# Dilated attention with moving values and a ones column, its sums swapped through DRAM, and half-split down weights in the experts

## Chip, cores and metric

The kernel runs on one core of a Trainium2 chip. The metric is the device time of one execution in microseconds, the median of several runs. Every time below is one of the kernel before the change.

## What is computed

One inference layer for 1024 prompt tokens and 8 single-token samples, all in fp32. Two parts of it matter here.

Dilated attention: 12 heads in three groups of 4, with windows (128, 512, 2048) and dilations (1, 4, 16); the three groups' results are joined by their log sums, which is the same as one softmax over the keys of all three.

```python
o = jnp.einsum('bnrhij,bnjrhd->bnirhd', p.astype(v.dtype), vv)     # per group
l = jnp.stack([r[1] for r in outs], axis=0)
w = jax.nn.softmax(l, axis=0)
return jnp.sum(w[..., None].astype(o.dtype) * o, axis=0)           # over the groups
```

Experts: every token goes to 2 of 32 experts, and the sorted tokens are worked off in blocks of 128 rows with one expert each.

```python
return (jax.nn.silu(xi @ w_gate[ei]) * (xi @ w_up[ei])) @ w_down[ei]   # xi: 128 x 1024
```

## The kernel before

The program is a row of stages, each with a barrier behind it: norm and projection, stick-breaking attention with the gates, dilated attention (`dilated`), the samples' attention, merge and residual, routing, experts (`experts`), and a last stage. Each engine has its own program in a stage, and the engines wait for each other by semaphores.

**`dilated`** works on two pairs of heads (a pair has one head in each half of the 128 partitions, `b` = 0 and 1). A pair has 16 units of 128 queries: units 0 to 7 are eight consecutive blocks of the undilated group with one or two key tiles, units 8 to 15 are the classes modulo 4 of each half of the sequence, for the two dilated groups together, with 2 or 4 key tiles. The order is written out by steps `s`: a unit's scores stand at step `score_step(a)`, its exponential 18 steps later (`EXP_LAG`), its transposes at 19 (`TURN_LAG`), its values at 20 and its eviction at 21; pair 1 starts 4 steps after pair 0's last scores. So pair 0's values run beside pair 1's scores.

Scores (L830) go to PSUM banks `S`; VectorE adds the bias, writes `row` and takes each query's maximum (L952). A query is in a different partition in the blocks and in the classes, so the maxima `mst` are exchanged through DRAM (`maxes`, L795 to L804, on SP's queue): the blocks' maxima out and in again by class, then the classes' out and in again by block. Four bytes or four times four at a time are moved. VectorE joins both (L927, L929), ScalarE takes the exponential with the joint maximum (L900). TensorE turns each 128 x 128 tile of `row` into `tp[b]` (L843), VectorE copies head 0's and ScalarE head 1's to `pT` (L935, L893), and TensorE multiplies, with the values as weights (64 columns) and `pT` moving, and once more with 64 columns of ones for the sums (L867). The result is `[64 dims | sums] x queries` in two banks `O`; ScalarE copies the blocks' to `acc` (L886), VectorE adds the classes' (L960). At a pair's end VectorE takes the reciprocal of all sums and multiplies (L964, L966).

All loads are issued by SP ahead of the swaps: 11 for each pair, of which 5 for the values (L779, L783), whose pieces are 512 bytes.

**`experts`** loops over 32 blocks in this run, with a lag of one block between each pair of steps. In a step TensorE does gate(n-1), turns the hidden tile of n-2, up(n-1), turns x of n, and down(n-2). Gate and up are three fp32r matmuls for each product, of operands split into a high part (rounded by ScalarE, L1930) and a low part (the rest, VectorE, L1973):

```python
def products(pe, out, w_high, w_low, m_high, m_low, first, last):
    pe.matmul(out, w_low, m_high, start=first, stop=False)
    pe.matmul(out, w_high, m_low, start=False, stop=False)
    return pe.matmul(out, w_high, m_high, start=False, stop=last)
```

Down is plain fp32 on `hT` and `wd` (L1891): 4 tiles of the hidden width by 2 banks of 512. The gate and up weights have one buffer each in two halves, reloaded as soon as VectorE has made the low part; `wd` has two. SP issues all of these loads, ScalarE issues the results.

Of the kernel before, what the change touches and what calls it, by code (L numbers as in the profile page):

```python
# [671 lines left out]
def dilated(nc, g):  # L672
# [6 lines left out]
    with ctx:  # L679
# [12 lines left out]
        EXP_LAG, TURN_LAG, VALUE_LAG, EVICT_LAG = 18, 19, 20, 21  # L692
# [24 lines left out]
        def keys(u, x, m):  # L717
# [9 lines left out]
        LAST = max(at_evict) + 1  # L727
# [3 lines left out]
        v = sb("v", [P, PAIRS, N_DIL, QT, P])  # L731
# [3 lines left out]
        acc = sb("acc", [P, PAIRS, 2, SEQ])  # L735
        ones = sb("ones", [P, HD])
        mst = sb("mst", [P, PAIRS, 2, UNITS])
        oth = sb("oth", [P, PAIRS, 2, UNITS])
        nm = sb("nm", [P, PAIRS, 2, UNITS])
        dist = row[:, 0, 0:BAND].bitcast(I32)  # L740
# [7 lines left out]
        s_full, row_full, joint_step, nm_full, p_full, tp_full, o_full, oa_read, ob_read, fin = map(sem, (  # L748
            "s_full", "row_full", "joint_step", "nm_full", "p_full", "tp_full", "o_full", "oa_read",
            "ob_read", "fin"))  # L750
        pT_full = [sem(f"pT_full{b}") for b in range(2)]
# [3 lines left out]
        m_in = [sem(f"m_in{p_}") for p_ in range(PAIRS)]  # L755
        ident, zT, ztok, oaT = g["ident"], g["zT"], g["ztok"], g["oaT"]
# [10 lines left out]

        @block.sync
        def _(sp):
            def load_qk(p_, x):  # L770
                c = x * PAIRS + p_
                sp.dma_start(q[:, p_, x, :], zT[c, :, 0:SEQ]).then_inc(qk_in[p_][x], 16)
                sp.dma_start(k[:, p_, x, :], zT[CA + c, :, 0:SEQ]).then_inc(qk_in[p_][x], 16)

            def load_v(p_):
                for x in range(N_DIL):
                    c = 2 * A_W + (x * PAIRS + p_) * P
                    if x == 0:
                        sp.dma_start(v[:, p_, x, :, :], ztok[0:SEQ, c:c + P].rearrange("(t p) n -> p t n", p=P))\  # L779
                            .then_inc(v_in[p_], 16)  # L780
                    else:
                        for h in range(2):
                            sp.dma_start(v[:, p_, x, h * STRIDE:(h + 1) * STRIDE, :],  # L783
                                         ztok[h * HALF:(h + 1) * HALF, c:c + P]
                                         .rearrange("(n r) c -> n r c", r=STRIDE)).then_inc(v_in[p_], 16)

            for p_ in range(PAIRS):
                for x in range(N_DIL):
                    load_qk(p_, x)
                load_v(p_)  # L790
            with nc.allow_non_contiguous_dma(reason="2048 maxima in another order"):
                for p_ in range(PAIRS):
                    sp.wait_ge(row_full, 2 * (p_ * UNITS + QT))
                    for b in range(2):
                        sp.dma_start(nat(p_, 0)[:, b, :], mst[:, p_, b, 0:QT]).then_inc(m_out[p_][0], 16)  # L795
                    sp.wait_ge(m_out[p_][0], 32)
                    for b in range(2):
                        sp.dma_start(by_class(oth, p_)[:, b, :, :], classes(p_, 0)[:, b, :, :]).then_inc(m_in[p_], 16)
                    sp.wait_ge(row_full, 2 * (p_ + 1) * UNITS)
                    for b in range(2):  # L800
                        sp.dma_start(classes(p_, 1)[:, b, :, :], by_class(mst, p_)[:, b, :, :]).then_inc(m_out[p_][1], 16)
                    sp.wait_ge(m_out[p_][1], 32)
                    for b in range(2):
                        sp.dma_start(oth[:, p_, b, 0:QT], nat(p_, 1)[:, b, :]).then_inc(m_in[p_], 16)  # L804

        @block.gpsimd
        def _(pool):
            pool.iota(dist[:, :], pattern=[[-1, BAND]], base=P, channel_multiplier=1).then_inc(drawn, 1)
            pool.memset(ones[:, :], 1.0).then_inc(drawn, 1)
# [10 lines left out]
        def _(pe):  # L820
# [15 lines left out]
            def turn(a):  # L836
                p_, u = place(a)
                for b in range(2):
                    pe.wait_ge(p_full, 2 * a + b + 1)
                    need(pe, pT_full[b], a)  # L840
# [3 lines left out]
                    last.then_inc(tp_full, 1)  # L844

            def values(a):
                p_, u = place(a)
                if u == 0:
                    pe.wait_ge(v_in[p_], 16 * 5)
                for b in range(2):  # L850
                    pe.wait_ge(pT_full[b], a + 1)
                if a >= 2:
                    e_, w = place(a - 2)
                    if w < QT:
                        pe.wait_ge(oa_read, e_ * QT + w + 1)
                    else:
                        pe.wait_ge(ob_read, e_ * QT + w - QT + 1)
                tiles = []
                for x, m in parts(u):
                    for t in range(m):  # L860
                        tiles.append((x, u + 1 - m + t if x == 0 else t * STRIDE + (u - QT) % STRIDE))
                for side in range(2):
# [898 lines left out]
def experts(nc, g):  # L1761
# [6 lines left out]
    with ctx:  # L1768
# [150 lines left out]
        def _(act):  # L1919
# [21 lines left out]
            def step(it, j):  # L1941
# [4 lines left out]
                if one:  # L1946
                    sigmoid(one[0])
# [444 lines left out]
```

## Time and profile before

| | |
|---|---|
| median of 3 runs | 2235.88 us (2226.49 to 2236.38) |
| profiled execution | 2228.89 us, of which the span is 2227.3 us |
| TensorE (PE) busy | 1855.4 us, 83% |
| VectorE (DVE) busy | 1057.1 us, 47% |
| ScalarE (ACT) busy | 800.7 us, 36% |
| mean granted TensorE clock | 0.911 of full |
| dilated attention | 787 to 984.6 us of the span |
| experts, first load to last issue | 1402.9 to 2041 us |

The profile is of one execution. A busy share is an average over all stages; which engine bounds is read stage by stage. PE rows are matmuls, PEld rows the weight loads, SPq, ACTq and POOLq the rows of queues. An fp32 matmul that isn't a transpose shows as two rows.

### The profile page before, as it was taken

The numbers are of one execution on the slowest core, as the hardware profiler recorded it, in microseconds if no ns is written. First come the engines' busy times: TensorE is split into PE (matmuls) and PEld (weight loads), VectorE is DVE, ScalarE is ACT, GpSimd is POOL, SyncE is SP. The second block draws the span as 40 slices with busy tenths as digits, with TensorE's granted clock in tenths as the row PEclk, the third lists the DMA queues.
The fourth block names the chain that finished last, engine by engine and source line by source line (L and its number), as shares of the span: only waits on it lengthen the run. The fifth ranks groups of instructions, "written<-read, shape, count | busy, mean of one in ns | idle before, by whom it ended". The sixth has DMA issues, their size and how long they took to land. (4 is left out here: it accounts for less than half of the span.)

```text
span 2227.3 us, 26881 instructions
## 1 busy us (share of the span) xinstructions
PE 1855.4 (83%) x9852; PEld 1443.3 (65%) x9852; DVE 1057.1 (47%) x1415; ACT 800.7 (36%) x1096; POOL 128.4 (6%) x181
## 2 busy tenths in 40 slices
PE   5999999789999947632498992599999999996698
PEld 4999999777777835431295541466666677773585
DVE  5211211158888733335151224466666666662674
ACT  4111111147666503220040000454555555452454
POOL 0111111100000000010031003000000000001110
PEclk7999999989999978675699995699999999998799
DMA  3443444245221160025354213899999999994620
GB/s 114 116 121 114 131 126 122 92 140 172 67 86 39 39 180 1 1 55 152 99 167 145 76 39 137 354 390 379 381 384 385 382 385 382 382 378 164 224 75 39
DMA packets 165325, 401.73 MB, mean 180 GB/s; under 512 B 25659, under 2 KB 102955, under 8 KB 144772
## 3 DMA queue, kind: packets, MB, share of 16 engines
q1 hardware_dynamic: 146004, 334.32, 41.8%
q0 software_dynamic: 10320, 33.82, 5.3%
q10 hardware_dynamic: 8928, 32.63, 3.6%
q8 instruction: 45, 0.74, 0.1%
q14 instruction: 28, 0.23, 0.0%
HBM read 325.80 MB, written 82.61 MB: 183 GB/s over the span
## 5 line engine op out<-in xcount | busy, mean ns | idle before, releaser
L87 PE MATMUL p_acc<-uh,p_wl 128*128 128x344 f32 x720 | 234.9, 326 | 13.0 <-DVE ul L293 9.0
L89 PE MATMUL p_acc<-uh,p_wh 128*128 128x344 f32 x720 | 230.6, 320 | 0.0
L88 PE MATMUL p_acc<-ul,p_wh 128*128 128x344 f32 x720 | 230.5, 320 | 0.0
L1891 PE MATMUL x_Y<-x_wd,x_hT 128*128 128x512 f32 x512 | 225.1, 593 | 0.8 <-DVE x_hT L1989 0.8
L305 DVE COPY p_zk<-p_tp 128x512 f32<-128x512 f32 (+1 forms) x90 | 44.2, 547 | 304.4 <-PE p_tp L226 304.4
L1973 DVE TENSOR_TENSOR x_wgl<-x_wg,x_wgh 128x2048 fp32r<-128x2048 f32 x64 | 143.9, 2290 | 49.8 <-ACT x_wgh L1930 49.8
L1891 PEld LDWEIGHTS x_Y<-x_wd,x_hT 128*128 128x128 f32 x512 | 95.0, 190 | 108.2 <-issue 107.1
L269 ACT ACTIVATE p_zc<-p_acc 128x344 f32<-128x344 f32 x90 | 41.2, 458 | 321.6 <-PE p_acc L89 321.6
L1973 DVE TENSOR_TENSOR x_wul<-x_wu,x_wuh 128x2048 fp32r<-128x2048 f32 x64 | 143.8, 2289 | 17.8 <-ACT x_wuh L1930 17.8
L87 PEld LDWEIGHTS p_acc<-uh,p_wl 128*128 128x128 f32 x720 | 135.8, 189 | 18.0 <-issue 14.9
L545 PE MATMUL g_acc<-uh,g_wl 128*128 128x344 f32 x384 | 129.1, 336 | 9.3 <-ACT u L576 7.1
L89 PEld LDWEIGHTS p_acc<-uh,p_wh 128*128 128x128 f32 x720 | 136.0, 189 | 0.0
L88 PEld LDWEIGHTS p_acc<-ul,p_wh 128*128 128x128 f32 x720 | 135.8, 189 | 0.0
L1930 ACT ACTIVATE x_wgh<-x_wg 128x2048 fp32r<-128x2048 f32 x64 | 118.8, 1905 | 47.2 <-DMA x_wg<-in_w_gate 47.2
L1505 PE MATMUL r_acc<-r_w,mT 128*128 128x512 f32 (+1 forms) x288 | 127.3, 601 | 10.1 <-DMA r_w<-in_w_out 10.1
L545 PE MATMUL g_acc<-ul,g_wh 128*128 128x344 f32 x384 | 127.4, 332 | 0.0
L545 PE MATMUL g_acc<-uh,g_wh 128*128 128x344 f32 x384 | 126.9, 330 | 0.0
L87 PE MATMUL x_G<-x_wgh,x_xl 128*128 128x512 f32 x256 | 114.0, 445 | 11.5 <-DVE x_xl L1967 11.5
L1930 ACT ACTIVATE x_wuh<-x_wu 128x2048 fp32r<-128x2048 f32 x64 | 118.5, 1901 | 0.3 <-DMA x_wu<-in_w_up 0.3
L1978 DVE TENSOR_TENSOR x_gs<-x_sg,x_G 128x512 f32<-128x512 f32 x32 | 22.1, 689 | 178.6 <-ACT x_sg L1923 178.6
L1505 PEld LDWEIGHTS r_acc<-r_w,mT 128*128 128x128 f32 (+1 forms) x288 | 51.6, 182 | 79.6 <-issue 69.2
L87 PE MATMUL x_U<-x_wuh,x_xl 128*128 128x512 f32 x256 | 102.9, 402 | 0.0
(316 smaller groups left out, 3676.8 us busy)
## 6 DMA issues: line engine op xcount, KB each, us to landing
x_wg<-in_w_gate SPq DMA_DIRECT2D x64, 1024.0 KB, 7.7
x_wu<-in_w_up SPq DMA_DIRECT2D x64, 1024.0 KB, 7.4
x_wd<-in_w_down SPq DMA_DIRECT2D x32, 2048.0 KB, 12.5
x_x<-xs SPq DMA_DIRECT2D x32, 512.0 KB, 11.6
ys<-x_y ACTq DMA_DIRECT2D x32, 512.0 KB, 11.8
zT<-p_zc ACTq DMA_DIRECT2D x30, 516.0 KB, 3.4
p_w<-in_w_in SPq DMA_DIRECT2D x30, 512.0 KB, 5.5
ztok<-p_zk POOLq DMA_DIRECT2D x30, 512.0 KB, 4.6
```

The costliest lines, as they stand in the source:

```text
L87: pe.matmul(out, w_low, m_high, start=first, stop=False)
L88: pe.matmul(out, w_high, m_low, start=False, stop=False)
L89: return pe.matmul(out, w_high, m_high, start=False, stop=last)
L269: act.activation(zc[:, b, s * NS:(s + 1) * NS], acc[b * NSPLIT + s][:, 0:NS], ACT.Copy).then_inc(zc_full, 1)
L305: dve.tensor_copy(zk[0:r, b, t0:t0 + m, :], tp[j % 2][0:r, 0:m, :]).then_inc(zk_full, 1)
L545: last = pe.matmul(acc[grp % 2][:, 0:NS], lhs[:, c % 2, kk, :], rhs[:, kk, t], start=(x == 0), stop=(x == M - 1), skip_group_check=True)
L1505: last = pe.matmul(acc[t % 2][0:r, c * 512:(c + 1) * 512], mT[:, k, t * P:t * P + r], w[:, k, c * 512:(c + 1) * 512], start=(k == 0), stop ...
L1891: last = pe.matmul(Y[c][:, :], hT[:, k, :], wd[:, b, k, c * 512:(c + 1) * 512], start=(k == 0), stop=(k == KF - 1))
L1930: act.activation(wh[:, HALVES[half], :], w[:, HALVES[half], :], ACT.Copy).then_inc(full, 1)
L1973: dve.tensor_tensor(wl[:, s, :], w[:, s, :], wh[:, s, :], ALU.subtract).then_inc(full, 1)
L1978: dve.tensor_tensor(gs[:, :], sg[:, :], G[:, :], ALU.mult).then_inc(gs_full, 1)
```

## The change

In `dilated` the operands of the value matmuls change places: the turned scores are now the weights (128 columns), and the values move, 64 dims with a column of ones beside them (`v` is 130 wide, a ones column at each end, so that each head has 65 columns with one of ones). The result is `queries x (sum, dims)` for each unit, all 32 of which ScalarE copies to `o` (L924). Blocks and classes are no longer added in the accumulator: their sums go to `den`, are swapped through DRAM as the maxima are, added, inverted, and `o` is scaled; then TensorE turns 4 units at a time into `tp[0]`, and VectorE copies (blocks) or adds (classes) into the output. VectorE makes both copies of each turned tile. SP loads only the queries and keys of pair 0; ScalarE's queue issues all the rest.

In `experts` the first two of the four hidden tiles of the down projection are computed like gate and up, in three fp32r matmuls, with high and low parts of `wd` and of the hidden tile; the other two stay fp32.

```diff
-        v = sb("v", [P, PAIRS, N_DIL, QT, P])
+        v = sb("v", [P, PAIRS, N_DIL, QT, WIDE])
@@ dilated, SP
+            for x in range(N_DIL):
+                load_qk(sp, 0, x)
+                swap(0, 0, mst, oth, m_out[0], m_in[0], row_full, 2 * QT, 2 * UNITS)
+                swap(1, 0, mst, oth, m_out[1], m_in[1], row_full, 2 * (UNITS + QT), 4 * UNITS)
+                for p_ in range(PAIRS):
+                    swap(p_, 2, den, osum, n_out[p_], n_in[p_], den_full, 2 * p_ + 1, 2 * p_ + 2)
@@ dilated, TensorE
-                if a >= 2:
-                    e_, w = place(a - 2)
-                    if w < QT:
-                        pe.wait_ge(oa_read, e_ * QT + w + 1)
-                    else:
-                        pe.wait_ge(ob_read, e_ * QT + w - QT + 1)
+                need(pe, o_read, a - 1)
                 for b in range(2):
-                    pe.wait_ge(pT_full[b], a + 1)
+                    pe.wait_ge(tp_read[b], turned[a, b][1] + 1)
+                            last = pe.matmul(O[a % 2][:, h], pT[:, a % 2, b, n * P:(n + 1) * P], v[:, p_, x, at_v, h],
+            def out(p_, n):
+                need(pe, tp_read[0], turned["out", (p_, n)][1])
+                pe.wait_ge(scaled, p_ + 1)
+                for t in range(4):
+                    last = pe.transpose(tp[0][:, t * P:(t + 1) * P], o[:, p_, n * 4 + t, 1:P + 1], ident[:, :])
@@ dilated, ScalarE
+            load_v(act, 0)
+            for x in range(N_DIL):
+                load_qk(act, 1, x)
+            load_v(act, 1)
@@ dilated, VectorE
+                    for b in range(2):
+                        dve.wait_ge(tp_full[b], turned[a, b][1] + 1)
+                        dve.tensor_copy(pT[:, a % 2, b, 0:n], tp[b][:, 0:n]).then_inc(tp_read[b], 1)
+                if s in at_scale:
+                    p_ = at_scale[s]
+                    dve.wait_ge(n_in[p_], 64)
+                    dve.wait_ge(den_full, 2 * p_ + 2)
@@ experts, ScalarE
+            def high_down(n, b, it):
+                act.wait_ge(d_in[b], it * 16 + 16)
+                need(act, d_used, n)
+                for k in range(KS):
+                    act.activation(wdh[:, k, :], wd[:, b, k, :], ACT.Copy).then_inc(dh_full, 1)
@@ experts, VectorE
+            def low_down(n, b):
+                for k in range(KS):
+                    dve.wait_ge(dh_full, n * KS + (k + 1))
+                    dve.tensor_tensor(wdl[:, k, :], wd[:, b, k, :], wdh[:, k, :], ALU.subtract).then_inc(dl_full, 1)
```

VectorE at the start of pair 1's values, where the new wait stands. Before, the turned tiles of head 0 follow the joint maximum (L927, L929) and its reciprocal and product (L964, L966); `u` is the memory that holds the output:

```order
L964 RECIPROCAL d_acc<-d_acc 128x1024
L966 TENSOR_TENSOR u<-d_acc 128x1024
L927 TENSOR_TENSOR d_oth<-d_oth,d_mst 128x32
L929 TENSOR_SCALAR d_nm<-d_oth 128x32
L935 COPY d_pT<-d_tp 128x128
L935 COPY d_pT<-d_tp 128x256 x10
```

After the change, at the same place:

```order
L951 TENSOR_TENSOR d_oth<-d_oth,d_mst 128x32
L953 TENSOR_SCALAR d_nm<-d_oth 128x32
L995 COPY d_den<-d_o 128x2x8
L971 COPY d_pT<-d_tp 128x128 x2
L971 COPY d_pT<-d_tp 128x256 x4
L1001 TENSOR_TENSOR d_den<-d_den,d_osum 128x32
L1003 RECIPROCAL d_osum<-d_den 128x32
L1006 TENSOR_TENSOR d_o<-d_o,d_osum 128x16x128
L959 COPY u<-d_tp 128x512
L971 COPY d_pT<-d_tp 128x256 x2
```

The sum of both `den` (L1001), which waits for pair 0's swapped sums, stands behind three units' copies and ahead of all others.

ScalarE at the end of the experts, from the last but one result on. Before, the results (L1935) and their issues (L1939) are all that is left behind the last sigmoid:

```order
L1923 ACTIVATE x_sg<-x_G 128x512
L1935 ACTIVATE x_y<-x_Y 128x512 x2
L1939 DMA ys<-x_y 128x1024
L1935 ACTIVATE x_y<-x_Y 128x512 x2
L1939 DMA ys<-x_y 128x1024
```

After the change:

```order
L1973 ACTIVATE x_sg<-x_G 128x512
L1990 ACTIVATE x_hh<-x_tph 128x256
L1995 ACTIVATE x_y<-x_Y 128x512 x2
L1999 DMA ys<-x_y 128x1024
L1986 ACTIVATE x_wdh<-x_wd 128x1024 x2
L1990 ACTIVATE x_hh<-x_tph 128x256
L1995 ACTIVATE x_y<-x_Y 128x512 x2
L1999 DMA ys<-x_y 128x1024
```

The last block's down weights are rounded (L1986) behind the result of the block before it.

## Rows read from the trace of the kernel before

**Rows 1.** The page's first line.
```profile
span 2227.3 us, 26881 instructions
```
**Rows 2.** Busy time by stretch: PE, PEld, DVE, ACT, POOL, then granted clock, DMA share, GB/s.
```profile
787.00:813.20 26.20, 18.83 (x96) 12.37 (x96) 17.87 (x81) 0.00 (x0) 2.24 (x7) 0.80 1.02 342
813.20:831.50 18.30, 0.00 (x0) 0.00 (x0) 0.05 (x2) 0.00 (x0) 0.00 (x0) 0.53 0.32 29
831.50:912.00 80.50, 61.14 (x486) 45.49 (x486) 24.02 (x89) 23.36 (x56) 0.00 (x0) 0.79 0.02 1
912.00:921.00 9.00, 0.00 (x0) 0.00 (x0) 8.93 (x7) 0.00 (x0) 0.00 (x0) 0.58 0.16 2
921.00:975.90 54.90, 42.16 (x390) 33.28 (x390) 11.64 (x25) 23.35 (x56) 0.00 (x0) 0.73 0.00 1
975.90:984.60 8.70, 0.00 (x0) 0.00 (x0) 8.38 (x3) 0.00 (x0) 0.00 (x0) 0.64 0.00 0
1430.00:1470.00 40.00, 37.58 (x155) 27.64 (x154) 28.37 (x20) 21.09 (x16) 0.00 (x0) 0.96 1.00 407
1441.00:2023.00 582.00, 582.00 (x2310) 407.74 (x2309) 364.26 (x242) 297.94 (x241) 0.00 (x0) 1.00 0.96 376
```
**Rows 3.** Timeline of one block of the experts: start, length, instruction.
```profile
1714.12 0.39 PE L87 MATMUL x_U<-x_wuh,x_xl 128*128 128x512 f32 x1
1714.35 0.39 PE L88 MATMUL x_U<-x_wul,x_xh 128*128 128x512 f32 x1
...
1717.05 7.03 PE L1891 MATMUL x_Y<-x_wd,x_hT 128*128 128x512 f32 x16
...
1730.10 3.71 ACT L1930 ACTIVATE x_wgh<-x_wg 128x2048 fp32r<-128x2048 f32 x2
```
**Rows 4.** Timeline of the tail of dilated attention.
```profile
976.54 6.55 DVE L964 RECIPROCAL d_acc<-d_acc 128x1024 f32<-128x1024 f32 x1
983.13 1.22 DVE L966 TENSOR_TENSOR u<-d_acc 128x1024 f32<-128x1024 f32 x1
```
**Rows 5.** Timeline of the end of the experts.
```profile
2031.66 7.12 PE L1891 MATMUL x_Y<-x_wd,x_hT 128*128 128x512 f32 x16 [0.80 <-DVE x_hT L1989]
2032.31 0.34 ACTq L1939 DMA_DIRECT2D ys<-x_y  x1
```
**Rows 6.** Timeline of pair 0's scores and first swap, VectorE and SP's queue.
```profile
800.40 0.08 DVE L952 DVE_READ_ACCUMULATOR2_ANT d_mst<- 128x1 f32 x1
...
811.51 3.80 SPq L795 DMA_DIRECT2D maxes<-d_mst  x2
824.83 0.87 SPq L798 DMA_DIRECT2D d_oth<-maxes  x2
...
831.46 0.19 DVE L927 TENSOR_TENSOR d_oth<-d_oth,d_mst 128x32 f32<-128x32 f32 x1 [18.25 <-DMA d_oth<-maxes]
```
**Rows 7.** Waits of SP's queue, 787 to 935: total, times, longest.
```profile
SPq L798 <- DMA maxes<-d_mst: 19.5, 2, 10.0
```
**Rows 8.** Timeline of TensorE in a wide unit of pair 1.
```profile
963.72 1.09 PE L843 MATMUL d_tp<-ident,d_row 128*128 128x128 f32 x8
965.85 1.09 PE L867 MATMUL d_O<-d_pT,d_v 128*64 128x128 f32 x16 [1.03 <-DVE d_acc L960]
...
967.74 1.09 PE L843 MATMUL d_tp<-ident,d_row 128*128 128x128 f32 x8
```
**Rows 9.** Timeline of the router: a narrow matmul on 128-column weights.
```profile
1323.32 1.87 PE L1522 MATMUL r_lg<-r_wr,r_u2T 128*128 128x36 f32 x16
```
**Rows 10.** The page's groups: weight loads of 128 fp32 columns.
```profile
L1891 PEld LDWEIGHTS x_Y<-x_wd,x_hT 128*128 128x128 f32 x512 | 95.0, 190 | 108.2 <-issue 107.1
```
**Rows 11.** Waits of the dilated stage, 787 to 985.
```profile
PE d_O L867 <- DVE d_acc L960: 17.5, 12, 2.3
```
**Rows 12.** Timeline of TensorE in wide units of pair 0.
```profile
897.01 1.98 PE L867 MATMUL d_O<-d_pT,d_v 128*64 128x128 f32 x16 [2.25 <-DVE d_acc L960]
...
905.72 1.15 PE L867 MATMUL d_O<-d_pT,d_v 128*64 128x128 f32 x16 [2.25 <-DVE d_acc L960]
```

More of the change, by code:

```diff
@@ L755, in dilated @@
         m_in = [sem(f"m_in{p_}") for p_ in range(PAIRS)]
+        n_out = [[sem(f"n_out{p_}{n}") for n in range(2)] for p_ in range(PAIRS)]
+        n_in = [sem(f"n_in{p_}") for p_ in range(PAIRS)]
         ident, zT, ztok, oaT = g["ident"], g["zT"], g["ztok"], g["oaT"]
@@ L787, in _, with swap @@
[L787 to L791, printed above, removed]
-                for p_ in range(PAIRS):
[L793 to L804, printed above, removed]
+            def swap(p_, at, src, dst, out_sems, in_sem, ready, first, second):
+                for b in range(2):
+                    if b == 0:
+                        sp.wait_ge(ready, first)
+                    sp.dma_start(nat(p_, at)[:, b, :], src[:, p_, b, 0:QT]).then_inc(out_sems[0], 16)
+                sp.wait_ge(out_sems[0], 32)
+                for b in range(2):
+                    sp.dma_start(by_class(dst, p_)[:, b, :, :], classes(p_, at)[:, b, :, :]).then_inc(in_sem, 16)
+                sp.wait_ge(ready, second)
+                for b in range(2):
+                    sp.dma_start(classes(p_, at + 1)[:, b, :, :], by_class(src, p_)[:, b, :, :]).then_inc(out_sems[1], 16)
+                sp.wait_ge(out_sems[1], 32)
+                for b in range(2):
+                    sp.dma_start(dst[:, p_, b, 0:QT], nat(p_, at + 1)[:, b, :]).then_inc(in_sem, 16)
@@ L806, in _ @@
+            for x in range(N_DIL):
+                load_qk(sp, 0, x)
+            with nc.allow_non_contiguous_dma(reason="2048 maxima and sums in another order"):
+                swap(0, 0, mst, oth, m_out[0], m_in[0], row_full, 2 * QT, 2 * UNITS)
+                swap(1, 0, mst, oth, m_out[1], m_in[1], row_full, 2 * (UNITS + QT), 4 * UNITS)
+                for p_ in range(PAIRS):
+                    swap(p_, 2, den, osum, n_out[p_], n_in[p_], den_full, 2 * p_ + 1, 2 * p_ + 2)
         @block.gpsimd
@@ L1941, in step @@
             def step(it, j):
-                one, three = lag(it, j, 1), lag(it, j, 3)
+                one, two, three = lag(it, j, 1), lag(it, j, 2), lag(it, j, 3)
                 new = it * 2 + j
@@ L1993, in step @@
                 new = it * 2 + j
+                if two:
+                    low_down(two[0], two[1])
                 if one:
@@ L2007, in end @@
                 last = np_ * 2 - 1
+                low_down(last - 1, 0)
                 gated(last)
@@ L2010, in end @@
                 hidden(last)
+                low_down(last, 1)
                 hidden_T(last)
```

197 lines of the change are left out of this document (120 added, 77 removed).

## The prediction

> **What bounds the kernel now.** I read the page first, then the busy time by stage, then the waits and the timeline of the two stages that the change touches. The span is 2227.3 us [rows 1] and the profiled execution took 2228.9 us, so 1.6 us lie around the span; the sum below is made against 2228.9. The three timed runs lie between 2226.5 and 2236.4, so it stands at their lower side. Less than about 0.5% (11 us) can't be told from no change.
>
> The stages follow one another with a barrier between them, so each is read alone [rows 2]. Dilated attention takes 197.6 us in six pieces: scores of pair 0 while its inputs stream in (26.2), an idle stretch with neither TensorE nor VectorE at work (18.3), pair 0's values beside pair 1's scores (80.5), a turnaround with only VectorE busy (9.0), pair 1's values (54.9), and a tail with only VectorE (8.7). No engine is full in any of them: it is a chain of short hand-overs. The experts stage is the opposite: from 1441 to 2023 TensorE is busy for 582.0 of 582.0 us at full granted clock, with a DMA share of 0.96. TensorE ends each block there, and DMA stands right behind it.
>
> **Experts.** A block has 76 rows of TensorE (48 for gate and up, 12 transposes, 16 for the down projection); 2310 rows in 582 us [rows 2] are 30.4 blocks, so a block takes 19.1 to 19.2 us. The down projection takes 7.03 us for 16 rows: 8 fp32 matmuls of 512 columns, two rows each, 0.44 us a row [rows 3]. The fp32r rows of the same width start 0.23 us apart [rows 3]. The change turns 4 of the 8 fp32 matmuls into 3 fp32r rows each: 4 x (2 x 0.437 - 3 x 0.227) = 0.77 us less per block, and 24.6 us over 32 blocks if TensorE stays the bound.
>
> What is added runs on ScalarE, two copies of 1024 (3.71 us for two of 2048 [rows 3], so 0.95 each) and one of 256 (0.35), and on VectorE, two subtractions of 1024 (a product of 1024 took 1.22 [rows 4], I take 1.2) and one of 256 beside a copy of half size (0.4 more). Per block ScalarE is idle for 9.3 us and VectorE for 7.2 (busy 297.9 and 364.3 of 582 us, over 30.4 blocks) [rows 2]; 2.3 and 2.8 us fit. The down weights' pieces stand at a step's start, where both engines wait for the gate product. The hidden tile's 0.35 us stands ahead of the next gate weights' rounding; the work that hides it is TensorE's up projection and transposes, which never waited. Without that cover it would cost 0.35 x 32 = 11 us, which goes into the range.
>
> At the stage's end the cover is gone. The last block's down weights can be rounded only once the block before has let go of the single buffer, and ScalarE first copies out that block's result and issues it, at 2032.3; before, the last down projection had begun at 2031.7 [rows 5]. Now come, from 2032.6, 0.95 + 0.95 us of copies, 0.35 for the hidden part and two VectorE steps of 0.4 with their hand-overs: 2037.1, so 5.4 us more. TensorE has by then idled over 6 us, and in the dilated stage's idle stretch the granted clock was 0.53 [rows 2], hence the last projection starts at half clock: 7 us of work, some 2.5 us longer. Experts: -24.6 + 5.4 + 2.5 = -17 us.
>
> Can DMA follow? 376 GB/s [rows 2] over 19.2 us are 7.2 MB a block; at 18.43 us that asks for 392 GB/s. The stretch from 1430 to 1470 moved 407 [rows 2], which would allow 17.7 us. So it fits, by 0.7 us.
> The Trainium skill (DMA: Bandwidth & Descriptors, Specifications) gives a core about 358 GB/s of HBM. The trace's 376 over 582 us is already above it. By the page's figure nothing could be won in this stage; by the row all of it.
>
> **Dilated attention, piece by piece.**
> *Loads and the first swap.* SP issued the first half of pair 0's maxima only at 811.5, behind 22 loads, though unit 7 had been reduced at 800.5; it read back at 824.8, and VectorE went on at 831.5, 6.6 us after [rows 6]. With the other loads on ScalarE's queue, SP is free for it at 800.5. The transfer has a latency of its own: SP waited 10.0 us for it once and 9.5 the other time, one of the two with nothing else under way [rows 7]. So it lands at 811 at the earliest and at 824.8, as before, at the latest. From the other side, the scores end at 813.2 and the second half needs 5.7 us: 819. I take 822.5 for VectorE's start, nearer the early end: -9 us (-12 to 0). That the scores begin perhaps 1 us later, since value rows share the DMA engines with the first keys, is in it.
>
> *Matmuls of the values.* Before, a unit of four tiles took 1.9 us at full clock in 32 rows [rows 8]. Now there are half as many matmuls, 65 columns wide, each with its own 128-column fp32 weights. The nearest rows are the router's: 36 columns on 128-column weights, 16 rows in 1.87 us [rows 9]. So 16 rows in 1.9 to 2.2 us: no gain, no loss. The bound above is a load that isn't hidden, 0.19 us a row [rows 10], so 3.0 us.
>
> *Pair 0's loop, 80.5 us.* The gain is a wait. In a wide unit (8.7 us) TensorE stands 2.25 us ahead of the values, because VectorE copies, reduces two score tiles and then adds into the accumulator; this wait came to 17.5 us in 12 places [rows 11, 12]. Now ScalarE empties the bank, and the first head's values begin after VectorE's first copy. For four wide units I count 2.2 us each, for the three ahead of them 1.9, and 0.2 for the others: -16 us (-8 to -20).
> *Turnaround, 9.0 us.* The reciprocal of 1024 (6.55) and the product (1.22) are gone [rows 4]; the swap's second half remains, 6.2: -3.
> *Pair 1's loop, 54.9 us.* A wide unit takes 4.0 us, 2.1 of them from the start of the turns to the values [rows 8]; now 3.6. With the other units that is -5. Against it: SP swaps the sums of pair 0 only after pair 1's maxima are through. The same chain, 10 + 1 + 3 + 3 us, ends some 20 us after the last score reduction. VectorE comes to this wait after the third unit, some 14 us after that reduction; queued behind it are all turned tiles, so TensorE stands 6 to 7 us. Then a sum, a short reciprocal and a product over 2048 (2 x 1.22) take 3 us, and four output tiles add transposes and a copy each, 1.9 us, through the one bank that also turns head 0: +7.6. Of these 17, 2 lie beside values: +15 - 5 = +10 us (+3 to +14; +3 if the transfer of scattered words is quick).
> *Tail, 8.7 us.* The last sums go out and come back, 5.7 us behind an eviction and a copy (0.8), then 3 us of scaling, then four times turn and copy with nothing beside it, 8: 17.5, so +9 us (+6 to +12).
> Dilated: -9 - 16 - 3 + 10 + 9 = -9 us.
>
> **Sum:** -17 - 9 = -26, so 2203 us.
>
> **Rivals.** *DMA is the bound in the experts stage.* For it: a share of 0.96, and only 0.7 us of room above. Against it: 407 GB/s in one stretch, and a TensorE that never waits for weights. The blocks stay at 19.2 us, only the end's 8 us are paid, and with -9 the time is 2228. I give it 0.17. The skill's 358 GB/s would be this case.
> *The weight loads of the values aren't hidden.* At 0.19 us a row against 0.12, 312 rows (156 tiles, two rows each) cost 22 us on TensorE's chain: 2225. At the stage's granted 0.79 [rows 2] it is 0.24 a row, 37 us, 2240: slower. It decides from 0.20 a row on, where the 26 us are eaten. Against it stand the router's rows. 0.08, of which 0.06 slower.
> *The swaps are quick:* the 10 us aren't paid where SP no longer stands behind loads. Then 3 us at the first, 7 at pair 0's sums, and 2 of the tail: 2191. 0.15.
> *The change doesn't do what it says in the dilated stage:* TensorE's wait for the accumulator only moves to the second copy of a turned tile on VectorE, which now makes both. Then the loops give 6 instead of 21 us, and the time is 2218. 0.10.
> My forecast has 0.50.
>
> **How the numbers follow.** The forecast's own terms span about 2192 to 2215. With the 11 us of the hidden part, the DMA case at 2228 and the quick swaps at 2191, 8 in 10 lie between 2182 and 2229. Faster by over 0.5% (under 2218): 0.50 + 0.15 + half of the 0.10, and 0.07 of the DMA case, where the blocks gain a part: 0.77. Slower: 0.06 and a little of the rest, 0.07. Within 0.5%: 0.16.
>
> **What would show it.** Blocks of 18.4 us with TensorE still full; idle time with DMA as releaser would be the first rival. The start and the granted clock of the last down projection. In the dilated stage: VectorE's joint maximum 35 us from the stage's start and not 44; wide units of pair 0 at 6.3 us; a wait of VectorE for the sums' return, 6 us long, after pair 1's third unit; a tail of 17 us; value rows 0.12 us apart at full clock.
> The prediction is wrong if blocks stay at 19.2 us, or if value rows stand 0.19 us apart.

## The result

The changed kernel takes 2243.3 us (median of 11 runs, 2235.0 to 2250.8), the kernel before 2230.8 in the same rounds (2223.7 to 2236.4): ratio 1.0062, 95% interval 1.0045 to 1.008. It is slower by 0.6%, where 2203 was forecast and 0.07 was given to slower.

The page's first line, against [rows 1]:
```profile
span 2239.3 us, 26891 instructions
```
Busy time by stretch of the changed kernel, against [rows 2]: loads and first swap, pair 0's loop, turnaround, pair 1's loop, tail, and most of the experts.
```profile
788.20:832.00 43.80, 19.05 (x96) 12.28 (x96) 18.36 (x82) 0.00 (x0) 2.39 (x10) 0.69 0.88 217
832.00:914.50 82.50, 77.55 (x330) 60.17 (x330) 27.63 (x97) 18.64 (x48) 0.00 (x0) 0.53 0.02 1
914.50:920.70 6.20, 0.00 (x0) 0.00 (x0) 0.51 (x5) 0.00 (x0) 0.00 (x0) 0.63 0.37 4
920.70:993.40 72.70, 54.40 (x250) 46.82 (x250) 20.39 (x42) 18.38 (x48) 0.00 (x0) 0.54 0.05 1
993.40:1010.40 17.00, 4.43 (x16) 2.86 (x16) 5.76 (x8) 0.26 (x1) 0.00 (x0) 0.54 0.08 1
1470.00:2023.00 553.00, 553.00 (x2391) 422.83 (x2390) 433.86 (x328) 364.21 (x328) 0.00 (x0) 1.00 0.98 392
```
The dilated stage grew from 197.6 to 222.2 us. Pair 0's loop is the row to look at: TensorE now works 77.6 of 82.5 us (61.1 of 80.5 before), so the wait for the accumulator is gone, and yet nothing was won, because the granted clock, whose two levels are 0.50 (1.2 GHz) and 1.00 (2.4 GHz), fell from 0.79 to 0.53 over the loop (the experiments below show that this is the cause). It stood at 0.50 up to the loop's last wide unit, for 77 us:
```profile
832.00:909.00 77.00, 73.25 (x306) 57.10 (x306) 24.53 (x89) 18.36 (x47) 0.00 (x0) 0.50 0.02 1
```
In pair 1's loop it fell from 0.73 to 0.54, and TensorE is idle for 18 of 72.7 us.

Timeline of the changed kernel, in the order of time: start, length, instruction, in brackets the idle time ahead and who ended it. These answer to [rows 6], [rows 12], [rows 3] and [rows 5].
```profile
802.80 1.00 SPq L809 DMA_DIRECT2D maxes<-d_mst  x2
825.06 0.88 SPq L812 DMA_DIRECT2D d_oth<-maxes  x2
825.98 0.98 SPq L815 DMA_DIRECT2D maxes<-d_mst  x2
831.80 0.19 DVE L951 TENSOR_TENSOR d_oth<-d_oth,d_mst 128x32 f32<-128x32 f32 x1 [16.43 <-DMA d_oth<-maxes]
...
893.73 3.65 PE L884 MATMUL d_O<-d_v,d_pT 128*128 128x65 f32 x16
...
918.56 1.20 SPq L809 DMA_DIRECT2D maxes<-d_den  x2
929.62 0.88 SPq L812 DMA_DIRECT2D d_osum<-maxes  x2
939.86 1.09 PE L893 MATMUL d_tp<-ident,d_o 128*128 128x128 f32 x4 [10.40 <-DVE d_o L1006]
991.37 1.97 PE L884 MATMUL d_O<-d_v,d_pT 128*128 128x65 f32 x16 [0.51 <-DVE d_pT L971]
...
1718.18 3.59 PE L1941 MATMUL x_Y<-x_wd,x_hT 128*128 128x512 f32 x8
2037.70 2.00 ACT L1986 ACTIVATE x_wdh<-x_wd 128x1024 fp32r<-128x1024 f32 x2 [1.23 <-issue]
2041.87 0.80 PE L87 MATMUL x_Y<-x_wdh,x_hl 128*128 128x512 f32 x1 [6.05 <-DVE x_hl L2059]
2042.46 0.63 PE L88 MATMUL x_Y<-x_wdl,x_hh 128*128 128x512 f32 x1
```
The same 16 value rows take 3.65 us at 893.7 and 1.97 at 991.4: the second stands in the one stretch of that loop where the clock is up. 1.97 lies within the 1.9 to 2.2 forecast from the router's rows [rows 9]. SP issued the first maxima 8.7 us sooner than before, but they were back only at 825.1, against 824.8 [rows 6]. Pair 0's sums go out at 918.6, behind pair 1's maxima, and cost TensorE 10.4 us. The experts did what was forecast: with TensorE full, 2391 rows in 553 us at 80 rows a block (48, 12, 12 and 8) are 18.5 us a block against 19.2, at 392 GB/s. At their end TensorE stands 6.05 us, and the next rows start 0.43 us apart instead of 0.23.

### The profile page after: what moved, and what is told of

Same layout as the page of the kernel before. It is cut to its first block and busy times, and to the rows that moved or that the text cites. A ratio compares the mean times of both kernels' runs of the same rounds, so it can differ in the third digit from the quotient of the medians.

```text
span 2239.3 us, 26891 instructions
## 1 busy us (share of the span) xinstructions
PE 1872.7 (84%) x9700; PEld 1502.3 (67%) x9700; DVE 1135.9 (51%) x1541; ACT 863.7 (39%) x1176; POOL 128.6 (6%) x184
## 5 line engine op out<-in xcount | busy, mean ns | idle before, releaser
L87 PE MATMUL p_acc<-uh,p_wl 128*128 128x344 f32 x720 | 234.8, 326 | 13.5 <-DVE ul L293 9.3
L2041 DVE TENSOR_TENSOR x_wul<-x_wu,x_wuh 128x2048 fp32r<-128x2048 f32 x64 | 143.8, 2289 | 17.8 <-ACT x_wuh L1980 17.8
L1941 PE MATMUL x_Y<-x_wd,x_hT 128*128 128x512 f32 x256 | 115.0, 592 | 0.0
L2064 DVE TENSOR_TENSOR x_wdl<-x_wd,x_wdh 128x1024 fp32r<-128x1024 f32 x64 | 75.5, 1221 | 77.5 <-ACT x_wdh L1986 77.5
L88 PE MATMUL x_G<-x_wgl,x_xh 128*128 128x512 f32 x256 | 101.2, 395 | 0.0
```

The costliest lines, as they stand in the source:

```text
L1941: last = pe.matmul(Y[c][:, :], hT[:, k - KS, :], wd[:, b, k, cols], start=False, stop=(k == KF - 1))
L2041: dve.tensor_tensor(wl[:, s, :], w[:, s, :], wh[:, s, :], ALU.subtract).then_inc(full, 1)
L2064: dve.tensor_tensor(wdl[:, k, :], wd[:, b, k, :], wdh[:, k, :], ALU.subtract).then_inc(dl_full, 1)
```

## The experiments

Sixteen kernels. "Before" was timed beside each; its medians lie between 2229.5 and 2233.3. "Joint" is VectorE's joint maximum, which opens a pair's loop; the loops below run from it to the pair's last value row. "-" and "+" are against the changed kernel where nothing else is said.

### Which part lost the time

**e1_experts_only.** The kernel before with the changed function `experts`.
```diff
-        hT = sb("hT", [P, KF, P])
+        KS = KF // 2
+        wdh, wdl = (sb(n, [P, KS, D], F32R) for n in ("wdh", "wdl"))
```


> The kernel before, with the experts' part of the change alone (gate and up untouched, half of each down projection split into high and low parts). By the two traces the experts' stage is 15.5 us shorter in the changed kernel (618.5 us against 634.0), and all that it loses it loses in dilated attention. If the two parts act apart, this kernel takes about 2231 - 15 = 2216 us, ratio 0.993. Rival: part of those 15.5 us came to the experts from the stages ahead of them (a later start with loads already under way), then it gains less than 10 us, ratio above 0.9955.

Measured: 2216.8 us, ratio 0.9931 (0.9903 to 0.9958), so -15 us against the kernel before. The parts act apart.

**e2_dilated_only.** The changed kernel with the function `experts` of before.
```diff
-        KS = KF // 2
-        wdh, wdl = (sb(n, [P, KS, D], F32R) for n in ("wdh", "wdl"))
+        hT = sb("hT", [P, KF, P])
```


> The kernel before, with the dilated part of the change alone; the experts as before. If the parts act apart, it takes 2243 + 15 = 2258 us, ratio to the kernel before 1.012, and its dilated stage is the 222 us of the changed kernel, with the granted clock at 0.53 in both loops. Rival as for the first kernel: the parts are not independent, and the ratio lies below 1.008.

Measured: 2258.2 us, ratio 1.0129 (1.0099 to 1.0159): the whole loss lies here. The clock of its loops was 0.59, not 0.53, and from the first joint maximum to the last output copy it took 173.5 us in the execution profiled (178.4 in the changed kernel's): with the same instructions the clock rose some 15 us sooner in pair 0's loop here.

### The clock

**e3_columns_130.** Each value matmul moves both heads' columns; the eviction picks.
```diff
-                            last = pe.matmul(O[a % 2][:, h], pT[:, a % 2, b, n * P:(n + 1) * P], v[:, p_, x, at_v, h],
+                            last = pe.matmul(O[a % 2][:, b * WIDE:(b + 1) * WIDE], pT[:, a % 2, b, n * P:(n + 1) * P], v[:, p_, x, at_v, :],
```


> The changed kernel, with each value matmul moving all 130 columns of its value tile (both heads and both ones columns) and not the 65 of its own head; the eviction picks the right 65 out of each half, so the output is the same. Theory: TensorE stays at half clock through both loops because the value matmuls keep it too little at work in the array (65 moved columns behind a weight load, 0.243 us a row). Then the granted clock of the loop over pair 0 rises from 0.53 to 0.7 or more, a value row costs 0.22 to 0.25 us at either width of time, transposes and scores run at double speed for part of the loop, and the kernel takes 2210 to 2235 us, less than the changed kernel in spite of twice the moved columns. Rival: the clock hangs on something else (the stage's rhythm, what went before the loop). Then it stays at 0.53, a value row of 130 columns takes about 0.43 us, 78 rows a pair cost 0.19 us more each, and the kernel takes 2243 + 30 = 2273 us.

Measured: 2212.9 us, ratio 0.9912 (0.9882 to 0.9942). Twice the moved columns, 30 us less. Busy time of e3's two loops, and one narrow unit of its timeline:
```profile
834.50:894.00 59.50, 51.95 (x324) 39.34 (x324) 26.11 (x95) 18.37 (x47) 0.00 (x0) 0.92 0.02 1
903.80:966.20 62.40, 39.84 (x250) 33.99 (x250) 20.23 (x43) 18.37 (x47) 0.00 (x0) 0.77 0.06 1
```
```profile
859.70 0.66 PE L868 MATMUL d_tp<-ident,d_row 128*128 128x128 f32 x4
860.81 1.13 PE L884 MATMUL d_O<-d_v,d_pT 128*128 128x130 f32 x8 [0.46 <-DVE d_pT L972]
```
The clock is back at 0.92 and 0.77, pair 0's loop takes 59.5 us instead of 79.5. Eight rows of 130 columns take 1.13 us at full clock; eight of 65 take 1.08 (next run): the second 65 columns are nearly free there.

**e5_warm_before_loop.** 65 columns; extra matmuls in the first swap's wait.
```diff
+                if at_joint.get(s - 2, -1) in (0,):
+                    warm((18, 2)[0])
+                    pe.wait_ge(m_in[at_joint[s - 2]], 64)
+                    warm((18, 2)[1])
```
Here `warm(n)` is n matmuls of `q[:, 0, 0, 0:512]` by `ident` into `tp[1]`.

> The changed kernel with 65 moved columns, and 20 extra matmuls (fp32, 512 moved columns, result never read) on TensorE while it waits for pair 0's first swap: 18 at once and 2 more when the swap has landed. They bring TensorE to full clock before the loop over pair 0 begins and take none of the path's time. Question: do the loop's own matmuls keep a clock that is already full? Theory A, they are too little work to hold it: the clock falls back to half within the first units, the loop still takes about 80 us and the kernel 2243 - 3 = 2240 us. Theory B, they hold it, they only can't raise it: the loop takes 55 to 62 us and the kernel about 2243 - 22 = 2221 us. If neither (the clock doesn't rise in the wait), the extra matmuls take 1.7 us each and the time is within 2 us of the changed kernel's.

Measured: 2225.8 us, ratio 0.9991 (0.9963 to 1.0019), 17.6 us under the changed kernel. Busy time of e5's extra matmuls and two loops, and a unit of its timeline:
```profile
814.10:829.80 15.70, 15.70 (x38) 6.75 (x36) 1.30 (x4) 0.00 (x0) 0.00 (x0) 1.00 0.80 94
830.50:887.00 56.50, 49.23 (x328) 37.62 (x328) 25.86 (x95) 18.37 (x47) 0.00 (x0) 1.00 0.03 1
900.70:972.90 72.20, 58.59 (x250) 50.80 (x250) 20.72 (x43) 18.36 (x47) 0.00 (x0) 0.50 0.04 1
```
```profile
837.76 1.08 PE L884 MATMUL d_O<-d_v,d_pT 128*128 128x65 f32 x8 [0.46 <-DVE d_pT L979]
```
Pair 0's loop, instruction for instruction that of the changed kernel, takes 56.5 us at clock 1.00. Pair 1's, which begins after a pause, takes 72.2 at 0.50. The same rows keep a full clock for 56.5 us here, and under a halved one they ran for 77 us without raising it: that is theory B's case, though its "can't raise" is too strong, since the clock did rise in the last wide units of both loops of the changed kernel (at about 909 and 988 us). (One of the ten runs, at 2243.5 us, had a mean clock of 0.895 against 0.904 to 0.911 in the others.)

**e7_and_warm**, on e6 (below), and **e9_warm_both_sums**, with 65 columns.
In e9 the sums of e4 are in as well:
```diff
+                if s - 2 in at_joint:
+                    p_ = at_joint[s - 2]
+                    first, then = ((18, 2), (6, 1))[p_]
```


> As the kernel with 130 columns and the sums ahead, with the 20 extra matmuls during the first swap as well. The first 10 us of the loop over pair 0, which ran at half clock with 130 columns too (granted clock 0.50 from 833 to 843), then run at full clock: about 4 us less, 2200 us. Rival: the wait between the last extra matmul and the first value rows (0.8 us and more) or the eviction and exp chain sets the pace of the first units, and it is within 1.5 us of the kernel without them.

> The changed kernel with its 65 moved columns, pair 0's sum swap issued ahead, and extra matmuls in both waits for a swap of maxima: 18 and 2 for pair 0, 6 and 1 for pair 1. After the run with extra matmuls ahead of pair 0 alone, in which the granted clock was 1.00 through the whole loop over pair 0 and 0.50 through that over pair 1, theory B says that the loop's own matmuls hold a full clock and can't raise a halved one. Then the loop over pair 1 runs at full clock as well (55 us instead of 72.7 less the 10.4 us of the late swap): 2226 - 10 - 8 = 2208 us, as good as 130 columns with the sums ahead (2203) within 5 us. Rival: pair 1's loop waits more often (the sums, the outputs), its clock falls in the first such wait and stays at half: 2217 us.

Measured: e7 2201.2 us, ratio 0.9881 (0.9845 to 0.9917), 1.5 us under e6, which their spreads (2197.9 to 2205.0 and 2198.3 to 2203.6) don't tell from none; e9 2213.7, ratio 0.9944 (0.9924 to 0.9965), not 2208. Both warmings ended too early. Timeline of e7 and then of e9:
```profile
833.52 3.42 PE L913 MATMUL d_tp<-d_q,ident 128*128 128x512 f32 x4 [4.24 <-DMA d_oth<-maxes]
```
```profile
892.96 5.42 PE L913 MATMUL d_tp<-d_q,ident 128*128 128x512 f32 x12
900.21 1.12 PE L913 MATMUL d_tp<-d_q,ident 128*128 128x512 f32 x2 [1.83 <-DMA d_oth<-maxes]
```
After a pause of 4.24 us the next rows cost twice as much (0.86 us each against 0.45); the clock of e7 was back up at about 837. In e9 the pause was 1.83 us, and pair 1's loop ran at 0.58. e9 missed its expectation by 6 us, and the half clock of that loop is in its trace. This left open whether 65 columns hold the clock in pair 1's loop at all.

**e14_65_warm_longer and e15_130_warm_longer**, both on e13 (below), with 65 and with 130 columns.
```diff
-                    first, then = ((18, 2), (6, 1))[p_]
+                    first, then = ((13, 3), (9, 3))[p_]
```


> As the kernel with all mended, but with 65 moved columns and extra matmuls in both waits, 13 and 3 for pair 0, 9 and 3 for pair 1, meant to leave no pause over 1 us ahead of either loop. Theory B (65 columns hold a full clock, and can't raise one): the granted clock is 0.95 or more in both loops; the value rows of 65 columns are a little cheaper than those of 130 and the first 10 us are warm, 2188 us. Rival: pair 1's loop, which stops for outputs and sums, falls back to half; then its loop costs about 10 us more and the kernel takes 2198 us.

> As the kernel with 65 columns and longer warming, with 130 columns. If the 65 columns hold the clock, the two take the same time within 3 us; if they fall back in pair 1's loop, this one is 7 to 10 us faster, since 130 columns raised the clock there by themselves within 5 to 10 us.

Measured: e14 2206.4 us, ratio 0.9888 (0.9854 to 0.9921); e15 2189.1, ratio 0.9803 (0.9772 to 0.9833). Pair 1's loop in e14, ahead of and behind the one pause at its first output tiles:
```profile
895.70:904.30 8.60, 7.23 (x38) 4.57 (x36) 3.29 (x12) 5.22 (x14) 0.00 (x0) 1.00 0.17 3
906.40:963.60 57.20, 51.08 (x220) 44.59 (x220) 15.42 (x31) 12.19 (x30) 0.00 (x0) 0.50 0.02 1
```
and the same two stretches of e15:
```profile
894.30:902.70 8.40, 7.05 (x38) 4.66 (x36) 3.10 (x12) 5.23 (x14) 0.00 (x0) 1.00 0.17 3
905.00:944.40 39.40, 29.72 (x220) 25.89 (x220) 14.81 (x31) 12.17 (x30) 0.00 (x0) 0.96 0.03 1
```
Both of these loops begin at full clock and both stop for about 2 us (904.3 to 906.4, and 902.7 to 905.0) until the scaled outputs are there. With 65 columns the clock stays down for the 57.2 us that are left; with 130 it comes back, and the same 220 rows take 39.4. The forecast for e14 named two cases, and it was the rival's, with more lost than it said: 17.8 us and not 10. Ahead of pair 0's loop e14's warming still left a pause of 3.68 us, and the first extra rows behind it fell to half clock. Later in that loop the clock fell without a pause ahead of it, for about 3 us in which TensorE did the eight score rows and the transposes of a wide unit, and came back:
```profile
875.70:878.60 2.90, 2.90 (x14) 1.88 (x10) 0.67 (x1) 0.00 (x0) 0.00 (x0) 0.50 0.10 3
```
The same happened in e9 (874.7 to 877.4). So 65 columns neither always hold the clock nor never raise it.

**e16_130_in_first_units**, on e13.
```diff
+                    wide = u < 6
+                    at_c = slice(0, WIDE) if wide else slice(b * (HD + 1), (b + 1) * (HD + 1))
```


> As the kernel with all mended, with 130 moved columns in the first six units of each pair alone and 65 in the other ten, and no extra matmuls. Theory B: in pair 0's loop the clock rises about 10 us after its start, as it did with 130 columns throughout, and stays up through the units of 65 columns; the time is within 3 us of the kernel with all mended. Rival: without the wide rows the clock falls back to half in the second half of the loop: 10 to 20 us slower.

Measured: 2197.1 us, ratio 0.9859 (0.9822 to 0.9896), 4.7 over e13: between the two forecasts, and the spreads overlap (2193.1 to 2209.6, and 2189.1 to 2199.0). The clock rose in the units of 130 columns and held in those of 65 but for about 3 us in a wide unit (878.8 to 882), 0.87 and 0.91 over the two loops (0.93 and 0.91 in e13).

**e12_before_warm.** The kernel before, with the extra matmuls of e5.
```diff
+                if at_joint.get(s - 2, -1) in (0,):
+                    warm((18, 2)[0])
+                    pe.wait_ge(m_in[at_joint[s - 2]], 64)
+                    warm((18, 2)[1])
```


> The kernel before, with the 20 extra matmuls in the wait for pair 0's first swap. In it the clock rises by itself 14 us into the loop over pair 0, so if a warm start is worth the same share there as elsewhere, those 14 us become 8 to 10 and the kernel gains 4 to 6 us: 2226 us. If the pace of that loop is set by the wait for the accumulator and not by TensorE, it gains less than 2 us.

Measured: 2227.9 us, ratio 0.9993 (0.9966 to 1.0021): no difference that can be told. In its profiled execution pair 0's loop took 70.0 us against 77.1, but its ten runs spread from 2215.0 to 2236.7. Whether the old loop gains by it stays open; e5's 17.6 us are not reached. That execution also gives the loop of before at nearly full clock (0.94). Two wide units of e12, with the wait for the accumulator between them, and then two of e5:
```profile
877.72 2.19 PE L830 MATMUL d_S<-d_k,d_q 64*128 64x256 f32 x8
883.18 1.09 PE L867 MATMUL d_O<-d_pT,d_v 128*64 128x128 f32 x16 [2.24 <-DVE d_acc L968]
885.08 2.20 PE L830 MATMUL d_S<-d_k,d_q 64*128 64x256 f32 x8
```
```profile
870.10 2.20 PE L854 MATMUL d_S<-d_k,d_q 64*128 64x256 f32 x8
875.72 2.20 PE L854 MATMUL d_S<-d_k,d_q 64*128 64x256 f32 x8
```
At full clock a wide unit takes 7.36 us before and 5.62 after the change.

### The swaps

**e4_sums_ahead**, and **e6_columns_and_sums**: the same with e3's 130 columns.
```diff
-                swap(1, 0, mst, oth, m_out[1], m_in[1], row_full, 2 * (UNITS + QT), 4 * UNITS)
-                for p_ in range(PAIRS):
-                    swap(p_, 2, den, osum, n_out[p_], n_in[p_], den_full, 2 * p_ + 1, 2 * p_ + 2)
+                both = ((1, 0, mst, oth, m_out[1], m_in[1], row_full, 2 * (UNITS + QT), 4 * UNITS),
+                        (0, 2, den, osum, n_out[0], n_in[0], den_full, 1, 2))
...
+                swap(1, 2, den, osum, n_out[1], n_in[1], den_full, 3, 4)
```
The first halves of `both` are written and read back together; then pair 1's second half, then pair 0's.

> The changed kernel, with pair 0's first sum swap issued on SP's queue ahead of the second half of pair 1's maxima swap, no longer behind it. Theory: the 10.4 us in which TensorE stands idle in the loop over pair 1 (929 to 940) are the sum swap of pair 0 that is started too late, since SP stands in program order behind the maxima of pair 1. Then that idle time shrinks to under 3 us and the kernel takes about 2234 us. Rival: the read-back of the sums is late whatever its place in the queue (its small writes take over 15 us), or what is taken from this wait comes back as a longer turnaround; then the time moves by less than 4 us. The clock of both loops stays at 0.53 by either.

> The 130 moved columns and pair 0's sum swap issued ahead, together. By the theory the two repair different losses, the clock (-30 us) and the late swap (-9 us, of which the faster loop leaves all, since the swap takes the same time), so the kernel takes about 2204 us, ratio to the kernel before 0.988. Rival: with the faster loop the swap of sums, whose latency is not TensorE's, stands on the path again in spite of its place, and only half of the 9 us comes: 2208 us or more.

Measured: e4 2234.2 us, ratio 1.0005 (0.9986 to 1.0024), -9; e6 2202.8, ratio 0.989 (0.9857 to 0.9924), -10 against e3. Waits of e4's dilated stage, total, times, longest:
```profile
PE d_tp L908 <- DVE d_o L1021: 10.6, 2, 9.3
```
and of the changed kernel's:
```profile
PE d_tp L893 <- DVE d_o L1006: 19.7, 2, 10.4
```
The 9.3 us left are the tail's; the other wait fell from 10.4 to 1.3.

**e8_loads_held** and **e10_v1_behind_swap.**
First e8's edit, then e10's:
```diff
+            act.wait_ge(m_out[0][0], 32)
             load_v(act, 0)
+            act.wait_ge(m_out[0][1], 32)
             for x in range(N_DIL):
                 load_qk(act, 1, x)
```
```diff
-            load_v(act, 1)
...
                 swap(0, 0, mst, oth, m_out[0], m_in[0], row_full, 2 * QT, 2 * UNITS)
+                load_v(sp, 1)
```


> The changed kernel, with ScalarE's loads held back: pair 0's values until the first half's maxima have landed in DRAM, pair 1's queries, keys and values until the second half's have. Theory: the first swap is slow (write issued at 803, landed at 819 to 825) because its small writes share the DMA engines with 6 MB of loads. Then the writes land in about 10 us, as those of the late sum swap do with nothing beside them (918.6 to 929.6), pair 0's first queries and keys come sooner as well, and the joint maxima come 6 to 8 us earlier: 2236 us. Rival: the swap's time is its own and not the loads'; then the joint maxima come within 2 us of before, pair 1's loads become late, and the kernel takes 2243 to 2250 us.

> The changed kernel, with the five loads of pair 1's values moved from ScalarE's queue to SP's, behind the whole first swap; all else as in the changed kernel. With the loads held until the writes had landed, the first write took 8.3 to 10.6 us instead of 15.9 to 21.8 and the second 4.7, but the last read-back, beside pair 1's loads, 11.7 us instead of 2.4. Theory: it is the transfers of values in many short pieces that keep the small writes of the swap waiting. Without those of pair 1 in its way the first write lands by 814, the joint maxima come at about 825 instead of 832, and the kernel takes 2237 us. Rival: the loads of queries and keys alone hold the write as long; then the joint maxima move by less than 3 us and so does the time.

Measured: e8 2242.5 us, ratio 1.0066 (1.0041 to 1.009), no gain; e10 2236.9, ratio 1.0043 (1.0022 to 1.0064), -6. Timeline of e8:
```profile
804.37 1.00 SPq L809 DMA_DIRECT2D maxes<-d_mst  x2
815.37 1.80 SPq L812 DMA_DIRECT2D d_oth<-maxes  x2
...
834.57 0.19 DVE L953 TENSOR_TENSOR d_oth<-d_oth,d_mst 128x32 f32<-128x32 f32 x1 [17.51 <-DMA d_oth<-maxes]
```
Timeline of e10:
```profile
800.86 1.00 SPq L809 DMA_DIRECT2D maxes<-d_mst  x2
815.94 0.88 SPq L812 DMA_DIRECT2D d_oth<-maxes  x2
816.86 0.98 SPq L815 DMA_DIRECT2D maxes<-d_mst  x2
820.26 0.99 SPq L818 DMA_DIRECT2D d_oth<-maxes  x2
823.21 0.19 DVE L951 TENSOR_TENSOR d_oth<-d_oth,d_mst 128x32 f32<-128x32 f32 x1 [9.65 <-DMA d_oth<-maxes]
```
From write to read-back the first half took 22.3 us in the changed kernel, 15.1 in e10 and 11.0 in e8 with no load beside it. In e8 the loads met the last read-back instead, so the joint maximum came at 834.6. In e10 it came at 823.2, the 822.5 of the prediction. Of these 8.6 us the timing shows 6. The wait only moved until pair 1's values, needed last, were the ones put behind.

### The end of the experts, and all together

**e11_experts_end**, on e1.
```diff
-                output(last - 1, 0, np_ - 1)
-                high_down(last, 1, np_ - 1)
+                high_down(last, 1, np_ - 1, spare[0], True)
                 high_hidden(last)
+                output(last - 1, 0, np_ - 1)
```
`spare` is the first half of each of `wgh` and `wgl`; VectorE and TensorE use it for the last block too.

> The experts' part of the change alone, with another end: the high and low parts of the last block's down weights go into the gate weights' split buffers, which nobody needs any more, while the block before is still being multiplied; and ScalarE copies the last block's hidden rows ahead of the output of the block before. In the changed kernel the last down projection starts 6.05 us after the work before it on TensorE and its first nine matmuls start 0.43 us apart instead of 0.23. By the theory the start comes about 4.7 us sooner, and if the shorter pause leaves the clock up 1.8 us are saved as well: 2216.8 - 5 to 7 = 2210 to 2212 us. Rival: the end of the experts is hidden behind what follows (the final stage's own loads), and the time stays at 2216 to 2217 us.

Measured: 2211.7 us, ratio 0.9934 (0.9908 to 0.996). The median is 5.1 us under e1's, but the ratios are the same, so the timing doesn't tell the two apart. Timeline of e11:
```profile
2012.96 0.47 PE L87 MATMUL x_Y<-x_wgh,x_hl 128*128 128x512 f32 x1 [1.65 <-ACT x_y L1959]
2013.27 0.39 PE L88 MATMUL x_Y<-x_wgl,x_hh 128*128 128x512 f32 x1
2013.49 0.39 PE L89 MATMUL x_Y<-x_wgh,x_hh 128*128 128x512 f32 x1
```
and of e1 at the same place:
```profile
2015.96 0.79 PE L87 MATMUL x_Y<-x_wdh,x_hl 128*128 128x512 f32 x1 [6.06 <-DVE x_hl L2019]
2016.55 0.63 PE L88 MATMUL x_Y<-x_wdl,x_hh 128*128 128x512 f32 x1
2016.98 0.63 PE L89 MATMUL x_Y<-x_wdh,x_hh 128*128 128x512 f32 x1
```
The pause is 1.65 us, not 6.06, and the rows after it stand 0.23 us apart, not 0.43: the clock stayed up. From the first load to the last result's issue the stage takes 614.7 us in e11's trace and 621.9 in e1's; that gain rests on the two traces alone.

**e13_all_mended.** e3, e4, e10 and e11 together.
```diff
+                load_v(sp, 1)
+        spare = [t[:, 0:KS * D // FE, :].rearrange("p (k a) f -> p k (a f)", k=KS) for t in (wgh, wgl)]
```


> The changed kernel with what the runs so far named mended together: 130 moved columns (-30 us alone), pair 0's sum swap ahead (-9 alone; with the columns -10), pair 1's value loads behind the first swap (-6), the new end of the experts (-5). If they add up, 2203 - 6 - 5 = 2192 us, ratio to the kernel before 0.983. Rival: the first swap's gain is hidden or the experts' stage, fed by DMA at its end, gives its 5 us back; then 2198 us or more.

Measured: 2192.4 us, ratio 0.9825 (0.98 to 0.9851). The parts add up to what was expected. With e15's warming it is 2189.1, 2.0% under the kernel before and, by the medians, 2.4% under the changed one.

## Why the prediction was wrong, point by point

- **Experts, -17 us: right.** -15.5 by the traces, -15 by e1. The blocks gained 0.7 us (0.77 forecast), DMA followed at 392 GB/s, and the end cost what was said: 6 us of pause, then half clock. e11's trace shows both taken back.
- **Pair 0's loop, -16 us: wrong, +2. This step failed.** The sum took a wait away and left every row at the price it had at the granted clock of before. The wait for the accumulator did go: TensorE is idle for 5 us of 82.5 instead of 19 of 80.5. But the change also cut what the value matmuls move, from 312 rows of 128 columns a pair to 156 of 65, and with that the clock no longer rose: 0.53 for 0.79. With 130 columns (e3) or a clock already up (e5) the loop takes 59.5 and 56.5 us, from joint to last value, against 77.1 before: 18 to 21 us less. Part of that is the clock again (0.92 and 1.00 for 0.79). Beside e12's loop, 70.0 us at 0.94, they are 10.5 and 13.5 us shorter. So the mechanism forecast is there, hidden by the clock, but its term was too large as well. The 17.5 us in 12 places [rows 11] are those of both loops; of pair 0's, from joint to last value, the trace of before says:
```profile
PE d_O L867 <- DVE d_acc L960: 11.4, 6, 2.3
```
  And a shorter wait, for VectorE's copy of the turned tile, stands in its place: 7.3 us in 16 places in e5, where before it was 4.8 in 8. A wide unit gained 1.7 us at full clock and not 2.2.
- **The rows' price: right at full clock, and the rival named the wrong cause.** 0.123 us a row in wide units, no dearer for its weights. The rival's 0.24 a row nearly came (3.65 us for 16, 0.228), but from the halved clock, and so not in the value rows alone: eight transposes take 1.97 us at half clock and 1.09 at full. Only the wide units' eight score rows take the same at both, 2.19 us at 905.08 and at 911.19. Its "slower, 2240" got the time nearly right by another mechanism.
- **First swap, -9 us: wrong, -1.** The write went out at 802.8, 14.6 us into the stage, where 13.5 and perhaps 1 more were forecast. Its latency was put near that of a swap with nothing else under way (10 us), and it went out among 6 MB of loads on the second queue. I had named 824.8 as the late bound and put the value near the early one. e10 shows that nearly all of it is there once pair 1's values wait: the joint maximum comes 8.6 us sooner.
- **Turnaround, -3, and tail, +9: right,** -2.8 and +8.3.
- **Pair 1's loop, +10 us: +17.8.** The late sums cost 10.4 us of idle time, not 6 to 7 (e4: 9 us come back), and the 4 us that are left fit the clock, 0.54 for 0.73; no run takes them apart. How much hangs on it there, e14 and e15 show with 17.8 us over the same 220 rows.

By the two profiled executions 38 us were missed: 18 in pair 0's loop, 8 in the first swap, 8 in pair 1's loop, 1 to 2 in the experts, and 3 outside both parts (the span grew by 12.0 us, the two stages by 24.6 - 15.5 = 9.1), which stay unexplained. The clock has the largest share. Most of pair 0's 18 us and some 4 of pair 1's are its; e3 gains 30 us by it, more than was missed there, because pair 0's loop then runs at a higher clock than before the change.

## What to carry to other kernels

A row's price belongs to a granted clock, so when an edit takes work off TensorE in a loop that isn't full, ask first whether the clock still rises with what is left; moving columns that nobody needs can be the cheaper kernel, and so can a few matmuls in a wait, if they reach to its end. A moved DMA issue is worth what its transfer meets on the way: look at which loads are under way at the new time, and put those needed last behind it. Where a single buffer is handed on at a stage's end, look for one that the stage has stopped using.

## What the runs showed of the hardware that I had not expected

- TensorE at half clock, busy 73.3 of 77.0 us (832 to 909), stayed at 0.50 and rose only in the loop's last wide unit, and the same instructions started at full clock kept it for 56.5 us with only 49.2 of them busy. So busy time doesn't tell which way it goes: two loops of equal code differ by 23 us by the clock they begin with. The Trainium skill (TensorE: Matmul & The Clock Gate, Part 1) says that the throttled state is the default and "activity releases the throttle". By that, so busy a loop should have come to full clock long before. The trace of the changed kernel does not agree, unless activity is something other than busy time. e3 moved more columns with the same number of rows, and the clock came up after some 9 us; no run here shows what is counted.
- The length of a pause doesn't tell either. Pauses of 1.83 (e9), 2.07 (e14), 2.30 (e15) and 4.24 us (e7) were followed by half clock, in e15 only 2.5 us after the work had resumed. One of 1.65 us (e11) left the clock up, and so did two of 2.2 us in e12, over both of which it stayed at 1.00:
```profile
880.90:890.50 9.60, 5.15 (x49) 3.79 (x48) 4.56 (x12) 3.64 (x6) 0.00 (x0) 1.00 0.00 0
```
  In e9 and e14 it fell for about 3 us with TensorE busy throughout.
- At full clock 8 value rows of 130 columns take 1.13 us, of 65 columns 1.08; at half clock 16 of 65 take 3.65.
- The first half's write, in pieces of one word, takes 11.1 us to its read-back with nothing beside it (918.56 to 929.62) and 22.3 beside loads; the second half's, in pieces of four words, 3.4 (816.86 to 820.26 in e10). A write in longer pieces might take most of the first swap's latency away; that wasn't tried.
